# Segment sums of a chunked scan moved to TensorE with a constant triangle, and small work moved into the projections beside it

## Chip, cores and metric

The kernel runs on one core of a Trainium2 chip. The metric is device time in microseconds (us) for one launch; lower is better. The engines of the core that matter here are TensorE (PE), VectorE (DVE), ScalarE (ACT) and GpSimd (POOL). Each runs its own list of instructions in order, and they meet only at semaphores.

## What is computed

A float32 model of three residual layers over 512 tokens of width 1024: sparse attention with a gated MLP, a Mamba-2 scan mixer (SSD) with a gated MLP, and a short-convolution mixer with a gated MLP. The change lies in the scan mixer alone. Of the reference this is the part:

```python
def step(state, inp):                       # one chunk of 128 tokens; 4 chunks
    x_k, dt_k, b_k, c_k = inp               # 32 heads of 64, in 4 groups
    acs = jnp.cumsum(dt_k * a_g, axis=1)
    seg = acs[:, :, None] - acs[:, None, :]
    lmat = jnp.exp(jnp.where(causal, seg, -jnp.inf))
    cb = jnp.einsum("blgn,bsgn->blsg", c_k, b_k)
    w = cb[..., None] * lmat * dt_k[:, None]
    y = jnp.einsum("blsgh,bsghp->blghp", w, x_k)
    y = y + jnp.einsum("blgn,bghpn->blghp", c_k, state) * jnp.exp(acs)[..., None]
    decay = jnp.exp(acs[:, -1:] - acs) * dt_k
    state = (state * jnp.exp(acs[:, -1])[..., None, None]
             + jnp.einsum("bsgn,bsgh,bsghp->bghpn", b_k, decay, x_k))
    return state, y
```

Around it: `dt = softplus(dt_raw + dt_bias)`; `y` plus a skip term is multiplied by `silu(z)`, normalised over each of the 4 groups (512 channels, root of the mean square), scaled, and projected by `w_out`.

## The kernel before

Activations lie with channels on the 128 partitions and the 512 tokens in the free dimension. Each projection is a `gemm` over panels of weights. A weight panel is loaded by a DMA (`raw`), ACT copies it to the rounded type (`whi`, `weight_hi`), DVE takes the remainder (`wlo`, `weight_lo`), and PE multiplies in three products per block (L663 to L665). `SSD_IN` has 41 tiles; tile 24 (`DT_AT`) carries dt, whose softplus runs over the next tiles. Tiles 25 to 40 are the gate z. `SSD_OUT` takes 16 contraction blocks (its operand `yhi`, `ylo`), and its first two output tiles are multiplied block by block as those blocks become ready.

Between these two projections stands the scan. It has 16 steps G = 4c + g (chunk c, group g), each of 8 heads, handled as two halves U = 2G and 2G + 1 of 4 heads, 512 columns wide. The order on each engine is written out by hand. Per step:

- PE `spread(G)`: the product C·B of the group into bank 6 (L967), then for every head a matmul of dt·a, broadcast along the columns, with the triangle `usum` (L979), eight in all. It leaves in bank 0 or 1 the cumulative sum along the columns, the same in every row.
- DVE `segments(G)`: from each of these 128x128 blocks it subtracts the row's own cumulative sum and adds the mask `smask` (L1894, eight instructions).
- ACT: copies C·B to `cbuf` (L1363), takes the exponent of the spread sums for c > 0 (`xbuf`, L1370) and of the segments (`ebuf` or `sqr`, L1371).
- DVE `weights(G)`: multiplies the exponents by `cbuf` (L1906, two instructions).
- POOL: for c > 0 multiplies `xbuf` by C (L597, two instructions), and for c < 3 makes `xdec`, the decayed inputs (L606).
- PE `outputs(G)`: eight matmuls of `xdt` with the weights (L999), and for c > 0 eight of `state` with `xbuf` (L1002), two heads side by side in the array.
- PE `states(G)`, c < 3: one float32 matmul of 512 columns (L1013) into bank 7.
- DVE `gated(G)`: adds the skip term (L1917, four), multiplies by the gate (L1922), then waits for `states(G)` and updates `state` (L1929, or L1931 and L1934).
- ACT squares the result (L1355), PE sums the squares (`group_sums`, L1024).

Once per chunk PE turns x (`turn_x`, L949) into banks 0 to 3 and B (`turn_b`, L958) into bank 4, and DVE makes `xdt` (L1880). `turn_x(c + 1, ...)` thus shares banks with the spread sums and the outputs. The triangle and mask are made by POOL after `SSD_IN`. dt is turned (L925) and summed (L935, L936) on PE after the last tile of `SSD_IN`. After the last step all 16 group sums go through one mean, root and reciprocal (L1961, L1384, L1964), are spread over the partitions (L1060, 16 matmuls), and DVE and ACT make the operand blocks (L1974, L1387, L1968).

Of the kernel before, what the change touches and what calls it, by code (L numbers as in the profile page):

```python
# [213 lines left out]
def build(nc, w8, w22, xT, params, heads, w_cmp, w_ada, out):  # L214
    with ExitStack() as ctx:
# [89 lines left out]
        btok = sb("btok", [P, 4, P], F32, at(24))  # L305
        ebuf = sb("ebuf", [P, 2, S], F32, at(26))
        usum = sb("usum", [P, P], F32, at(30))
        smask = sb("smask", [P, P], F32, at(30.5))
# [102 lines left out]
        s_lb = sem("cumsums_spread")  # L411
        s_ein = sem("segments_made")
# [114 lines left out]
        def _(pool):  # L527
# [6 lines left out]
            chain(pool.memset(pcmp[:, :, :, :, :], 0.0))  # L534
            chain.wait()
            chain(pool.affine_select(out=ident[:, :], in_=ident[:, :], compare_op=ALU.not_equal, fill=1.0,
# [18 lines left out]
            def ada(half):  # L555

                for s in range(ADA_HALF * half, ADA_HALF * (half + 1)):
                    acc = ada_acc[:, s % 2, :]
                    for k in range(KD):
# [3 lines left out]
                        if k == 0:  # L563
                            if s >= 2:
# [14 lines left out]
            pool.wait_ge(s_pe, START["SSD_IN"] + 41)  # L579
            chain(pool.memset(usum[:, :], 1.0))  # L580
            chain(pool.memset(smask[:, :], 0.0))
            chain.wait()
            chain(pool.affine_select(out=usum[:, :], in_=usum[:, :], compare_op=ALU.is_ge, fill=0.0,
                                     base=0, pattern=[[1, P]], channel_multiplier=-1))
            chain(pool.affine_select(out=smask[:, :], in_=smask[:, :], compare_op=ALU.is_ge, fill=NEG,
                                     base=0, pattern=[[1, P]], channel_multiplier=-1))
            chain.wait()
            pool.memset(small[:, 31:32], 0.0).then_inc(s_const, 1)

            for c in range(NT):  # L590
                tok = slice(c * P, (c + 1) * P)
                for g in range(4):
                    for u in (2 * g, 2 * g + 1) if c else ():

                        pool.wait_ge(s_xe, 8 * (c - 1) + u + 1)
                        b = xbuf[:, u % 4, :].rearrange("p (a l) -> p a l", a=4)
                        pool.tensor_tensor(b, b, cv[:, 4 + g, tok].unsqueeze(1).to_broadcast([P, 4, P]),  # L597
                                           ALU.mult).then_inc(s_cx, 1)
                    if c < NT - 1:

                        pool.wait_ge(s_xd, 4 * c + g + 1)
                        pool.wait_ge(s_dec, 1)
                        if c > 0:
                            pool.wait_ge(s_st, 4 * (c - 1) + g + 1)
# [1560 lines left out]
```

## Time and profile before

| | us |
|---|---|
| median of 3 runs | 2294.11 (2292.66 to 2294.92) |
| the profiled execution | 2289.19 |
| its span, first to last instruction | 2287.5 |
| PE busy in the span | 2165.6 (95%) |
| DVE, ACT, POOL busy | 1309.2, 818.7, 293.2 |
| end of `SSD_IN` on PE to first block of `SSD_OUT` | 1019.8 to 1182.8 |

The profile has one execution. A busy PE is not a PE at its peak: the granted clock (PEclk, 1.00 is 2.4 GHz and 0.50 is 1.2 GHz) says how fast it was. A float32 matmul appears as two records, since it passes the array in two parts; "x16" records are thus eight matmuls. Matmuls overlap at their ends, so the distance from start to start tells what one costs. Idle time marked "issue" is a wait whose end the profile ties to no other engine.

### The profile page before, as it was taken

How to read it: one execution, taken by the hardware profiler on the slowest of the kernel's cores; microseconds unless marked ns; L12 is line 12 of the kernel's file. 1: busy time of each engine (PE TensorE's matmuls, PEld its weight loads, DVE VectorE, ACT ScalarE, POOL GpSimd, SP SyncE). 2: the span in 40 equal slices, each digit the busy share in tenths (PEclk: the TensorE clock that was granted, in tenths of full speed). 3: DMA queues.
4: the chain of work that ended last, by engine and by line, in shares of the span. 5: the costliest groups of instructions: out<-in, count | busy, mean ns of one | idle time of the engine just before them, and what ended most of it. 6: DMA issues, size and time to landing. Idle time of an engine off the chain costs nothing.

```text
span 2287.5 us, 27332 instructions
## 1 busy us (share of the span) xinstructions
PE 2165.6 (95%) x10704; PEld 1747.0 (76%) x10704; DVE 1309.2 (57%) x2222; ACT 818.7 (36%) x1324; POOL 293.2 (13%) x201
## 2 busy tenths in 40 slices
PE   7999988999999999997789999999989999999997
PEld 6866666888888778876678788888878877888885
DVE  4277754777754687638883587765455544333333
ACT  4156652544431354423242354442231223222221
POOL 0000000100049600002310200009800000000000
PEclk9999999999999999998899999999979988999998
DMA  8110002232245322220003122326512322222321
GB/s 272 50 47 20 20 10 65 84 101 92 93 150 200 116 96 102 92 93 1 1 1 111 65 102 93 100 86 212 192 47 92 101 65 73 93 92 94 94 92 53
DMA packets 59791, 203.58 MB, mean 89 GB/s; under 512 B 6800, under 2 KB 7312, under 8 KB 59408
## 3 DMA queue, kind: packets, MB, share of 16 engines
q1 hardware_dynamic: 55920, 191.36, 25.5%
q10 hardware_dynamic: 3744, 10.49, 1.4%
q8 instruction: 85, 1.39, 0.2%
q14 instruction: 42, 0.34, 0.0%
HBM read 197.63 MB, written 2.10 MB: 87 GB/s over the span
## 4 chain that ended last, share of the span: by engine, by line
PE 86%; DVE 6%; ACT 4%; issue 2%; POOL 1%; DMA 0%; DVEq 0%; SPq 0%; POOLq 0%; ACTq 0%
PE bank L663 25%; PE bank L664 25%; PE bank L665 25%; PE bank L618 2%; ACT pbuf L1244 2%; DVE pbuf L1681 1%; PE bank L766 1%; PE bank L861 1%; PE bank L815 1%; PE bank L838 1%; PE bank L645 1%; PE bank L979 1%; POOL h L553 1%; ACT pt L1261 1%; PE bank L1013 1%
## 5 line engine op out<-in xcount | busy, mean ns | idle before, releaser
L663 PE MATMUL bank<-xhi,whi 128*128 128x512 f32 x1712 | 685.6, 400 | 29.3 <-DVE xlo L1456 23.0
L664 PE MATMUL bank<-xlo,whi 128*128 128x512 f32 x1712 | 680.9, 398 | 0.0
L665 PE MATMUL bank<-xhi,wlo 128*128 128x512 f32 x1712 | 680.2, 397 | 0.0
L1444 DVE TENSOR_TENSOR wlo<-raw,whi 128x1024 fp32r<-128x1024 f32 (+1 forms) x322 | 412.6, 1283 | 367.8 <-ACT whi L1101 367.3
L1101 ACT ACTIVATE whi<-raw 128x1024 fp32r<-128x1024 f32 (+1 forms) x322 | 334.2, 1041 | 770.0 <-PE bank L665 709.5
L663 PEld LDWEIGHTS bank<-xhi,whi 128*128 128x128 f32 x1712 | 324.0, 189 | 110.7 <-issue 13.5
L665 PEld LDWEIGHTS bank<-xhi,wlo 128*128 128x128 f32 x1712 | 323.7, 189 | 79.8
L664 PEld LDWEIGHTS bank<-xlo,whi 128*128 128x128 f32 x1712 | 324.1, 189 | 77.0
L663 PE MATMUL bank<-hid_hi,whi 128*128 128x512 f32 x528 | 209.5, 397 | 0.0
L664 PE MATMUL bank<-hid_lo,whi 128*128 128x512 f32 x528 | 208.6, 395 | 0.0
L665 PE MATMUL bank<-hid_hi,wlo 128*128 128x512 f32 x528 | 208.5, 395 | 0.0
L665 PEld LDWEIGHTS bank<-hid_hi,wlo 128*128 128x128 f32 x528 | 99.0, 187 | 24.2
L663 PEld LDWEIGHTS bank<-hid_hi,whi 128*128 128x128 f32 x528 | 99.0, 188 | 23.9
L664 PEld LDWEIGHTS bank<-hid_lo,whi 128*128 128x128 f32 x528 | 99.0, 188 | 23.6
L571 POOL TENSOR_TENSOR ada_acc<-ada_acc,ada_w 128x768 f32<-128x768 f32 x56 | 115.8, 2069 | 4.7
L1560 DVE TENSOR_TENSOR upad<-bank,rstd_b 128x512 f32<-128x512 f32 x88 | 60.6, 691 | 78.3 <-PE bank L665 71.2
L553 POOL TENSOR_TENSOR h<-tmp,h 128x512 f32<-128x512 f32 x24 | 38.0, 1619 | 493.2 <-DVE tmp L1487 493.2
L1159 ACT ACTIVATE tmp<-upad,par 128x512 f32<-128x512 f32 x88 | 70.5, 803 | 27.0 <-DVE upad L1560 26.9
L1244 ACT ACTIVATE pbuf<-pbuf,stat 128x512 f32<-128x512 f32 (+3 forms) x128 | 70.2, 551 | 24.7 <-DVE stat L1684 24.7
L566 POOL TENSOR_SCALAR ada_acc<-ada_w,csil 128x768 f32<-128x768 f32 x8 | 12.2, 1527 | 510.3 <-DMA ada_w<-w_ada 510.3
L568 POOL TENSOR_SCALAR ada_w<-ada_w,csil 128x768 f32<-128x768 f32 x56 | 75.0, 1340 | 0.8 <-DMA ada_w<-w_ada 0.8
L1572 DVE SCALAR_TENSOR_TENSOR tmp<-upad,par,tmp 128x512 f32<-128x512 f32 x88 | 66.2, 752 | 3.1
(269 smaller groups left out, 2558.8 us busy)
## 6 DMA issues: line engine op xcount, KB each, us to landing
raw<-w SPq DMA_DIRECT2D x298, 512.0 KB, 3.6
ada_w<-w_ada SPq DMA_DIRECT2D x64, 384.0 KB, 3.1
raw<-w SPq DMA_DIRECT2D x24, 384.0 KB, 3.4
h<-xT ACTq DMA_DIRECT2D x8, 256.0 KB, 9.7
w_k<-w_cmp ACTq DMA_DIRECT2D x1, 2048.0 KB, 9.6
w_v<-w_cmp ACTq DMA_DIRECT2D x1, 2048.0 KB, 8.2
out_t<-h ACTq DMA_DIRECT2D x8, 256.0 KB, 2.0
dk<-stg ACTq DMA_DIRECT2D x2, 256.0 KB, 6.9
```

Of the source, the lines that this page charges most:

```text
L553: pool.tensor_tensor(h[:, j, :], tmp[:, j % 2, :], h[:, j, :], ALU.add).then_inc(s_h, 1)
L568: chain(pool.tensor_scalar(w, w, csil[:, k:k + 1], 1.0, ALU.mult, ALU.mult))
L571: pool.tensor_tensor(acc, acc, w, ALU.add).then_inc(s_ada_k, 1)
L663: pe.matmul(bk, whi[w][:, cols], hi[:, k, :], start=k == 0, stop=False)
L664: pe.matmul(bk, whi[w][:, cols], lo[:, k, :], start=False, stop=False)
L665: return pe.matmul(bk, wlo[w][:, cols], hi[:, k, :], start=False, stop=last)
L1101: act.activation(whi[g % SLOTS][:, 0:n], raw[g % RAWS][:, 0:n], ACT.Copy).then_inc(s_hi, 1)
L1159: act.activation(tmp[:, c % 2, :], upad[:, c % 2, 2:2 + S], ACT.Identity, scale=col("ffn_w", 3 * k + 2), bias=col("ffn_b", k)).then_inc(s_ ...
L1244: act.activation(pbuf[:, s % 3, g, 0:n], pbuf[:, s % 3, g, 0:n], ACT.Exp, scale=QSCALE, bias=stat[:, b, 4 + g:5 + g], accum_out=stat[:, b, ...
L1444: dve.tensor_tensor(wlo[g % SLOTS][:, 0:n], raw[g % RAWS][:, 0:n], whi[g % SLOTS][:, 0:n].bitcast(F32), ALU.subtract).then_inc(s_lo, 1)
L1560: dve.tensor_tensor(upad[:, c % 2, 2:2 + S], in_bank(c)[:, :], rstd_b[:, :], ALU.mult)\
L1572: ins = dve.scalar_tensor_tensor(out=tmp[:, v, :], in0=upad[:, v, 0:S], scalar=col("ffn_w", 3 * k), in1=tmp[:, v, :], op0=ALU.mult, op1=AL ...
```

## The change

- Segments on PE. ACT now writes the terms (`terms`): for each head the constant triangle `usum` times that head's dt·a, a copy with a per-partition scale, eight 128x128 instructions per step into four buffers `vbuf`. One matmul with the constant strictly lower triangle `after` turns the terms of four heads, 512 columns, into finished segments (`segments`, L985 in the new file). For c > 0 a second matmul of the same terms with `ones` gives the spread cumulative sums (`spread_cumsums`, L991).
- DVE loses the eight segment instructions; masking moves into C·B, which DVE multiplies by `usum` while copying it to `cbuf` (`causal_cb`, one 128x128 instruction). ACT loses that copy.
- x is turned step by step, two steps ahead, into bank 4 alone, and B into the same bank; B has two buffers. `keep_state` is a step of its own after `x_dt(G + 2)`. `gated(G)` comes in step G instead of a step later, and writes over `cv` rather than `tmp`.
- dt: `turn_dt` stands before tile 32 of `SSD_IN`, `cumulate` before tile 35, and DVE's copies of them between its tiles. The constants are made by POOL at the start of the kernel.
- Group norm: groups 0 to 2 are finished first; the sum of the last step, and the spread of group 3, are put before contraction blocks 4 and 8 of `SSD_OUT`.
- POOL's work per step is the same, with `xdec` ahead of the products with C.

PE, the last step of chunk 0 and what leads to chunk 1. `ident,cv` are the turns of x and B, `xdec,btok` the state products. Before:

```order
L999 MATMUL bank<-ebuf,xdt 64x128 x8
L1013 MATMUL bank<-xdec,btok 128x512
L1024 MATMUL bank<-ones,tmp 128x1 x4
L949 MATMUL bank<-ident,cv 128x128 x8
L999 MATMUL bank<-sqr,xdt 64x128 x8
L967 MATMUL bank<-cv 128x128
L979 MATMUL bank<-usum,dtk 128x128 x8
L1013 MATMUL bank<-xdec,btok 128x512
L949 MATMUL bank<-ident,cv 128x128 x8
L958 MATMUL bank<-ident,cv 128x128 x4
```

And now, one step:

```order
L985 MATMUL bank<-vbuf_122,after 128x512
L985 MATMUL bank<-vbuf_123,after 128x512
L1030 MATMUL bank<-ones,tmp 128x1 x4
L1008 MATMUL bank<-sqr,xdt 64x128 x8
L991 MATMUL bank<-vbuf_122,ones 128x512
L991 MATMUL bank<-vbuf_123,ones 128x512
L964 MATMUL bank<-ident,cv 128x128 x4
L974 MATMUL bank<-cv 128x128
L1021 MATMUL bank<-xdec,btok_117 128x512
```

Eight narrow matmuls became two of 512 columns, two more of 512 columns came in, and the turns are spread one group a step, behind the outputs.

DVE, two steps of chunk 1. `ebuf`/`sqr` times `cbuf` are the weights. Before:

```order
L1894 SCALAR_TENSOR_TENSOR ebuf<-bank,acs,smask 128x128 x8
L1917 SCALAR_TENSOR_TENSOR tmp<-cv,par,bank 128x128 x4
L1922 TENSOR_TENSOR zb<-zb,tmp 128x4x128
L1931 TENSOR_TENSOR state<-state,acs 128x512
L1934 TENSOR_TENSOR state<-state,bank 128x512
L1906 TENSOR_TENSOR ebuf<-ebuf,cbuf 128x512 x2
L1894 SCALAR_TENSOR_TENSOR sqr<-bank,acs,smask 128x128 x8
```

And now, one step:

```order
L1954 TENSOR_TENSOR ebuf<-ebuf,cbuf 128x512 x2
L1964 SCALAR_TENSOR_TENSOR cv<-cv,par,bank 128x128 x4
L1968 TENSOR_TENSOR zb<-zb,cv 128x4x128
L1938 TENSOR_TENSOR xdt<-bank,dtk 128x512
L1945 TENSOR_TENSOR cbuf<-bank,usum 128x128
```

The eight segment instructions are gone; one narrow one and one turn's `xdt` came in, and the weights stand ahead of the gate instead of behind the state.

The diff, cut to its core (removed functions are printed above):

```diff
--- before.py
+++ after.py
...
+        after = sb("after", [P, P], F32, at(130))
+        vbuf = [sb("vbuf0", [P, S], F32, where["ssum"]), sb("vbuf1", [P, S], F32, at(127.5)),
+                sb("vbuf2", [P, S], F32, at(124.25)), sb("vbuf3", [P, S], F32, at(120))]
...
-            gemm("SSD_IN", xhi, xlo, s_ev, EV["SSD_IN"], Q_SSD_PRE, freed=out_ring_left("DOWN1"))
...
+            gemm("SSD_IN", xhi, xlo, s_ev, EV["SSD_IN"], Q_SSD_PRE, freed=out_ring_left("DOWN1"),
+                 between=[((DT_AT + 8, 0), turn_dt), ((DT_AT + 11, 0), cumulate)])
...
+                if g == 0 and c < NT - 1:
+                    pe.wait_ge(s_bt, c + 1)
+                elif G:
+                    pe.wait_ge(s_xd, G)
...
-                for v in range(2):
...
-                    for k in range(4):
-                        hd = 8 * g + 4 * v + k
-                        mm = pe.matmul(bank[v][:, k * P:(k + 1) * P],
-                                       dtk[:, c, 1, hd:hd + 1].to_broadcast([P, P]), usum[:, :],
-                                       start=True, stop=True)
-                    mm.then_inc(s_lb, 1)
+            def segments(G):
+                for U in (2 * G, 2 * G + 1):
+                    pe.wait_ge(s_vm, U + 1)
+                    if U >= 10:
+                        pe.wait_ge(s_xe, U - 2 - 8 + 1)
+                    elif U >= 2:
+                        pe.wait_ge(s_ee, U - 1)
+                    pe.matmul(bank[U % 2][:, :], after[:, :], vbuf[U % 4][:, :], start=True, stop=True).then_inc(s_lb, 1)
+            def spread_cumsums(G):
+                for U in (2 * G, 2 * G + 1):
+                    pe.wait_ge(s_ee, U + 1)
+                    pe.matmul(bank[U % 2][:, :], ones[:, :], vbuf[U % 4][:, :], start=True, stop=True).then_inc(s_lx, 1)
...
+            for G in range(4 * NT):
+                c, g = G // 4, G % 4
+                if G + 1 < 4 * NT:
+                    segments(G + 1)
+                if G >= 2:
+                    if G == 2:
+                        pe.wait_ge(s_acv, 1)
+                    group_sums(G - 2)
+                outputs(G)
+                if G + 1 < 4 * NT and G + 1 >= 4:
+                    spread_cumsums(G + 1)
+                if G + 2 < 4 * NT:
+                    if g == 2 and c + 1 < NT - 1:
+                        turn_b(c + 1)
+                    turn_x(G + 2)
+                    products_cb(G + 2)
+                if c < NT - 1:
+                    states(G)
+            group_sums(4 * NT - 2)
+            pe.wait_ge(s_gn, 2)
+            pe.wait_ge(s_xe, 8 * (NT - 1))
+            pe.wait_ge(s_ee, 8 * NT)
+            pe.wait_ge(s_xd, 4 * NT)
+            for g in range(3):
+                spread_group(g)
+            pe.wait_ge(s_yk, 4 * NT)
...
+            def last_sums():
+                group_sums(4 * NT - 1)
+            def last_spread():
+                pe.wait_ge(s_gn, 4)
+                spread_group(3)
+            gemm("SSD_OUT", yhi, ylo, s_m, MV["SSD_OUT"], post=Q_SSD_POST, freed=[[]] * 4,
+                 between=[((None, 4), last_sums), ((None, 8), last_spread)])
...
+            def terms(G):
+                c, g = G // 4, G % 4
+                for v in range(2):
+                    U = 2 * G + v
+                    if U >= 12:
+                        act.wait_ge(s_lx, U - 4 - 8 + 1)
+                    elif U >= 4:
+                        act.wait_ge(s_lb, U - 4 + 1)
+                    for k in range(4):
+                        hd = 8 * g + 4 * v + k
+                        ins = act.activation(vbuf[U % 4][:, k * P:(k + 1) * P], usum[:, :], ACT.Copy,
+                                             scale=dtk[:, c, 1, hd:hd + 1])
+                    ins.then_inc(s_vm, 1)
...
+            def segment_exps(G):
+                for U in (2 * G, 2 * G + 1):
+                    act.wait_ge(s_lb, U + 1)
+                    if U >= 4:
+                        act.wait_ge(s_y, U - 3)
+                    act.activation(segs(U), bank[U % 2][:, :], ACT.Exp).then_inc(s_ee, 1)
...
+            terms(0)
+            keep_b(0)
+            segment_exps(0)
+            terms(1)
...
+                if G + 1 < 4 * NT:
+                    segment_exps(G + 1)
+                if G + 2 < 4 * NT:
+                    terms(G + 2)
+                if G + 1 < 4 * NT and G + 1 >= 4:
+                    cumsum_exps(G + 1)
+                if g == 2 and c + 1 < NT - 1:
+                    keep_b(c + 1)
+                if G >= 1:
+                    group_square(G - 1)
+            act.activation(small[:, 13:14], small[:, 12:13], ACT.Sqrt)
...
+            act.activation(gst[:, 1, 0:12], gst[:, 0, 0:12], ACT.Sqrt).then_inc(s_gr, 1)
             for j in range(NZ):
+                if j == 6:
+                    act.wait_ge(s_gn, 3)
+                    act.activation(gst[:, 1, 12:16], gst[:, 0, 12:16], ACT.Sqrt).then_inc(s_gr, 1)
...
+                if c == DT_AT + 9:
+                    dve.wait_ge(s_dtp, 1)
...
+                if c == DT_AT + 12:
+                    dve.wait_ge(s_ac, 1)
...
-            def segments(G):
...
-                    for k in range(4):
-                        hd = 8 * g + 4 * v + k
-                        ins = dve.scalar_tensor_tensor(
-                            out=segs(U)[:, k * P:(k + 1) * P], in0=bank[v][:, k * P:(k + 1) * P],
-                            scalar=acs[:, 0, c, hd:hd + 1], in1=smask[:, :], op0=ALU.subtract, op1=ALU.add)
-                    ins.then_inc(s_ein, 1)
+            def causal_cb(G):
+                dve.wait_ge(s_cb, G + 1)
+                dve.tensor_tensor(cbuf[:, G % 2, :], bank[6][:, 0:P], usum[:, :], ALU.mult).then_inc(s_cbk, 1)
...
+            dve.wait_ge(s_dtk, 1)
+            x_dt(0)
+            causal_cb(0)
+            causal_cb(1)
             weights(0)
+            x_dt(1)
+            dve.wait_ge(s_cv, 40)
             dve.wait_ge(s_dec, 1)
             for G in range(4 * NT):
...
+                if G + 1 < 4 * NT:
                     weights(G + 1)
-                    continue
-                gated(G - 1)
+                gated(G)
+                if G + 2 < 4 * NT:
+                    x_dt(G + 2)
+                    causal_cb(G + 2)
                 if c < NT - 1:
-                    x_dt(c + 1, 0)
...
+                    keep_state(G)
...
+            mean_squares(slice(0, 12), 4 * NT - 1)
+            inverse_roots(slice(0, 12), 1)
             for j in range(NZ):
                 g = j // 4
+                if j == 5:
+                    mean_squares(slice(12, 16), 4 * NT)
+                if j == 8:
+                    inverse_roots(slice(12, 16), 2)
```

## Rows read from the trace of the kernel before

**Rows 1.** Windows of the scan: us, busy us per engine, PEclk, DMA share, GB/s
```profile
1021.00:1030.00 9.00, 7.20 (x39) 7.23 (x40) 5.10 (x9) 2.29 (x4) 3.07 (x4) 0.67 0.17 61
1030.00:1060.00 30.00, 24.11 (x195) 20.42 (x193) 25.06 (x70) 7.96 (x16) 1.07 (x2) 0.93 0.00 1
1060.00:1097.00 37.00, 27.17 (x224) 23.19 (x224) 30.31 (x62) 12.02 (x24) 16.73 (x12) 0.82 0.00 1
1097.00:1138.00 41.00, 30.11 (x233) 25.34 (x232) 33.93 (x71) 12.30 (x25) 16.72 (x12) 0.82 0.00 1
1138.00:1175.00 37.00, 29.34 (x291) 26.49 (x291) 30.21 (x70) 12.98 (x27) 10.89 (x8) 0.92 0.00 1
```

**Rows 2.** Timeline in chunk 1: start, duration, instruction, [idle before and releaser]
```profile
1076.41 0.69 DVE L1934 TENSOR_TENSOR state<-state,bank 128x512 f32<-128x512 f32 x1
...
1077.20 2.05 PE L1013 MATMUL bank<-xdec,btok 128*128 128x512 f32 x2 [5.79 <-issue]
```

**Rows 3.** Waits between 1021 and 1183: waiting <- releaser: us, times, longest
```profile
PE bank L1013 <- issue: 25.1, 6, 5.8
```

**Rows 4.** Timeline of PE where it ran at the full clock without waiting
```profile
1097.05 0.49 PE L967 MATMUL bank<-cv 128*128 128x128 f32 x2
...
1097.37 1.95 PE L979 MATMUL bank<-usum,dtk 128*128 128x128 f32 x16
...
1099.16 1.02 PE L1013 MATMUL bank<-xdec,btok 128*128 128x512 f32 x2
...
1100.02 1.04 PE L949 MATMUL bank<-ident,cv 128*128 128x128 f32 x8
...
1101.33 0.95 PE L1024 MATMUL bank<-ones,tmp 128*128 128x1 f32 x8
...
1162.16 0.45 PE L999 MATMUL bank<-ebuf,xdt 128*64 128x128 f32 x4 [1.31 <-DVE zb L1922]
...
1164.09 1.05 PE L1024 MATMUL bank<-ones,tmp 128*128 128x1 f32 x8
```

**Rows 5.** Timeline from the end of SSD_IN to the first outputs
```profile
1019.51 0.40 PE L665 MATMUL bank<-xhi,wlo 128*128 128x512 f32 x1
...
1021.60 1.28 ACT L1347 ACT_TABLE_LOAD   x1
...
1022.80 0.38 PE L935 MATMUL bank<-dtk,usum 128*128 128x32 f32 x2 [2.28 <-DVE dtk L1860]
...
1034.71 1.09 PE L999 MATMUL bank<-ebuf,xdt 128*64 128x128 f32 x16
```

**Rows 6.** ACT: two scaled copies in a row (timeline), and a narrow plain one (groups)
```profile
8.68 0.71 ACT L1192 ACTIVATE xhi<-h,par 128x512 fp32r<-128x512 f32 x1
9.29 1.04 ACT L1101 ACTIVATE whi<-raw 128x1024 fp32r<-128x1024 f32 x1
...
L1363 ACT ACTIVATE cbuf<-bank 128x128 f32<-128x128 f32 x16 | 4.4, 272 | 16.4 <-PE bank L967 16.4
```

**Rows 7.** DVE in the scan by tile: count, ns minimum/median/maximum, first and last start
```profile
L1894 DVE SCALAR_TENSOR_TENSOR sqr<-bank,acs,smask x64: 335/340/351, 1034.9 to 1164.3; 128x128 f32<-128x128 f32 x64
L1880 DVE TENSOR_TENSOR xdt<-bank,dtk x16: 677/682/692, 1026.3 to 1150.6; 128x512 f32<-128x512 f32 x16
L1906 DVE TENSOR_TENSOR sqr<-sqr,cbuf x16: 677/686/1755, 1036.9 to 1167.9; 128x512 f32<-128x512 f32 x16
L1922 DVE TENSOR_TENSOR zb<-zb,tmp x16: 691/692/1659, 1041.6 to 1172.6; 128x512 f32<-128x512 f32 x16
L1931 DVE TENSOR_TENSOR state<-state,acs x8: 684/1109/1526, 1074.8 to 1144.1; 128x512 f32<-128x512 f32 x8
```

**Rows 8.** The end of the scan: timeline, then two groups by tile
```profile
1171.33 1.05 PE L1024 MATMUL bank<-ones,tmp 128*128 128x1 f32 x8
...
L663 PE MATMUL bank<-yhi,whi x128: 393/396/477, 1182.8 to 1272.7; 128*128 128x512 f32 x128
...
L1974 DVE SCALAR_TENSOR_TENSOR zb<-zb,par,bank x16: 740/744/751, 1179.8 to 1198.2; 128x512 f32<-128x512 f32 x16
```

More of the change, by code:

```diff
@@ L534, in _ @@
             chain(pool.memset(pcmp[:, :, :, :, :], 0.0))
+            chain(pool.memset(usum[:, :], 1.0))
+            chain(pool.memset(after[:, :], 1.0))
             chain.wait()
+            chain(pool.affine_select(out=usum[:, :], in_=usum[:, :], compare_op=ALU.is_ge, fill=0.0,
+                                     base=0, pattern=[[1, P]], channel_multiplier=-1))
+            chain(pool.affine_select(out=after[:, :], in_=after[:, :], compare_op=ALU.is_ge, fill=0.0,
+                                     base=-1, pattern=[[-1, P]], channel_multiplier=1))
             chain(pool.affine_select(out=ident[:, :], in_=ident[:, :], compare_op=ALU.not_equal, fill=1.0,
@@ L578, in _ @@
             add_update(KD)
[L579 to L596, printed above, removed]
+            for n in range(-1, 4 * NT):
+                c, g = (n + 1) // 4, (n + 1) % 4
+                if c >= NT:
+                    continue
+                if c < NT - 1:
+                    pool.wait_ge(s_xd, n + 2)
+                    pool.wait_ge(s_dec, 1)
+                    if c:
+                        pool.wait_ge(s_st, n - 2)
+                    hs = slice(8 * g, 8 * g + 8)
+                    pool.tensor_tensor(xdec[:, hs, :], xdt[:, hs, :],
+                                       acs[:, 1, c, hs].unsqueeze(2).to_broadcast([P, 8, HD]),
+                                       ALU.mult).then_inc(s_xdec, 1)
+                if c:
+                    tok = slice(c * P, (c + 1) * P)
+                    for U in (2 * n + 2, 2 * n + 3):
+                        pool.wait_ge(s_xe, U - 8 + 1)
+                        b = xbuf[:, U % 4, :].rearrange("p (a l) -> p a l", a=4)
@@ L688, in gemm @@
                             continue
+                        for (t, at_block), extra in between:
+                            if t is None and at_block == off + kb:
+                                extra()
                         pe.wait_ge(s_xt, XT[name] + off + kb + 1)
@@ L700, in gemm @@
                 for t in range(lead, n):
+                    for (tile, _), extra in between:
+                        if tile == t:
+                            extra()
                     bank_free(t)
@@ new lines, in cumulate @@
+            def cumulate():
+                pe.wait_ge(s_dtk, 1)
+                for c in range(NT):
+                    dta = dtk[:, c, 1, :]
+                    pe.matmul(bank[5][:, c * SH:(c + 1) * SH], usum[:, :], dta, start=True, stop=True)
+                    mm = pe.matmul(bank[5][:, (NT + c) * SH:(NT + c + 1) * SH], ones[:, :], dta, start=True, stop=True)
+                mm.then_inc(s_ac, 1)
+            gemm("SSD_IN", xhi, xlo, s_ev, EV["SSD_IN"], Q_SSD_PRE, freed=out_ring_left("DOWN1"),
+                 between=[((DT_AT + 8, 0), turn_dt), ((DT_AT + 11, 0), cumulate)])
```

249 lines of the change are left out of this document (82 added, 167 removed).

## Prediction

> **What bounds the kernel now.** I read the time by stage first, then the waits inside the stage that changes, then single instructions. Outside the scan PE is busy at the full clock and nothing of the change lies there but small pieces. From the end of `SSD_IN` (1019.8) to the first block of `SSD_OUT` (1182.8) the kernel spends 163.0 us. There PE is busy 24.1 of 30, 27.2 of 37, 30.1 of 41 and 29.3 of 37 us, at a granted clock of 0.93, 0.82, 0.82 and 0.92, while DVE is busy 25 to 34 us of each [rows 1]. So DVE's chain sets the pace and PE pays twice: it waits, and behind a wait it runs at half rate. In [rows 2] the reader sees one such place. PE idled 5.79 us ahead of the state product L1013, whose turn came when DVE had finished the state of the group before (1076.41 + 0.69 = 1077.10), and the product then took 2.05 us at the 1.2 GHz level, where the same pair takes 1.02 at 2.4 [rows 4]. These waits are 25.1 us in all, six of them [rows 3]; the clock behind them costs more. First outputs begin at 1034.7 [rows 5], the last end at 1171.3 [rows 8]: 136.6 us for 16 steps, 8.5 us a step.
>
> **What DVE loses.** Per step 8 segment instructions of 0.34 (start to start 0.27), 2.2 us, go [rows 7]. One narrow product with the triangle comes in, 0.29 as I estimate from the 0.34 row. Left are two weights 2 x 0.68, gate about 1.1 + 0.69, `xdt` 0.68, `causal_cb` 0.29, state 0.68 in chunk 0 or 0.69 + 0.69 later [rows 7]: 4.8 us in chunk 0 and 5.5 in chunks 1 and 2.
>
> **What ACT gains.** Eight 128x128 copies with a scale per partition. The narrow plain copy lasts 0.272. The scaled one of 512 columns lasts 0.71 and lets the next start after 0.61 [rows 6]. So each costs between 0.17 (0.27 less the 0.10 of overlap) and 0.37 (0.27 plus 0.10 for the scale, no overlap); I take 0.27, nearest to the narrow row: 2.2 us a step, bounds 1.4 and 3.0. With two exponents (0.6 each, four in c > 0) and the square, ACT works 4.1 us a step in chunk 0 and 5.3 later, 6.1 at the upper bound.
>
> **What PE does now.** Start-to-start costs at full clock [rows 4]: C·B 0.32; old spread sums 1.79; state product 0.86 (0.9 with the gap behind it); four turns 0.87 to 0.95; square sums 0.95; outputs 1.93 in c > 0, and 1.09 in chunk 0 [rows 5]. A float32 matmul of 512 columns is the same form as L1013, so the two segment matmuls are 1.8, as dear as the eight they replace. The two with `ones` in c > 0 are new: 1.8 x 12 steps = 21.6 us more PE work. Summed by the new order, from the start of the first outputs:
> steps 0 to 3: 3.3 (its segments are before it), 5.1, 7.0 (with one turn of B), 7.8 (spread sums of step 4 begin);
> steps 4 to 11: 1.8 + 0.95 + 1.95 + 1.8 + 0.95 + 0.32 + 0.9 = 8.67 each, with one more turn of B 70.3;
> steps 12, 13: 7.77 each; step 14: 6.5; step 15: 2.9.
> Together 118.4 us. Known waits on top: two turns that wait for ACT to copy B (0.8 each), and the last outputs, which follow their own spread sums by only 0.95 us while ACT and POOL still have to work on them, 1.0. That is 121.0.
>
> **Does anything else stop PE?** Through one step of 8.67: segments end at 1.8; ACT's exponents at 2.5, its terms for the next step at 4.7 (5.5), which PE wants at 8.67; outputs end at 4.7; spread sums at 6.5, exponents at 7.1, wanted free at 8.67; POOL's products with C end near 9.2, wanted at 11.4. DVE: weights by 3.3, gate 4.8 to 6.6, `xdt` behind the turn (7.5) to 8.2, state behind its product (8.7) to 10.2, next weights wanted much later. All other engines have one to three us in hand. So PE is the bound and has no gap of over about 1 us. Its clock then is 1.00; I take that because the windows without such gaps have it.
>
> **The start.** The last `SSD_IN` matmul moves back by the two pieces put between tiles, 2.3 us (today 1022.80 to 1025.1 for the sums [rows 5], part of it at half rate). In exchange the wait of 2.28 on DVE is gone. But ACT's last gate tile, its table load of 1.28 [rows 5] and the exponent of the sums now stand ahead of `terms(0)`: 1025.6, first terms 1026.8, second 1027.9. PE has idled about 4 us and gets half rate, as it did after 1022 (0.67 in [rows 1]): segments 1026.9 to 1030.4, turn to 1032.2, `xdt`, `causal_cb`, second C·B, weights, and the next segments, first outputs at 1036.5. That is 1.8 us later than now. Were the clock full, it would be 1034 to 1035.
>
> **The end.** Last outputs at 1036.5 + 121.0 = 1157.5, against 1171.3. Today 11.5 us follow until `SSD_OUT` begins. Two rounds of square and sum (the sum is 1.05 [rows 8]) and one of four spreads go from ahead of it, near 4 us earlier. It is given back: at block 4 PE sums the last step's squares (0.95), DVE stands waiting for that sum before block 5 and only then makes the remainder of block 4, so PE stalls about 1.7; the last spread costs 0.9. DVE makes a block in (1198.2 - 1179.8)/15 = 1.23 and PE takes 1.41 for one (two output tiles, from 128 triples in 89.9 us) [rows 8], so DVE does not catch the stall up, and PE does not stall again. 4 - 3.5 is 0 to 1; I put 0. POOL's constants at the kernel's start are hidden by the first weight load.
>
> **Sum.** 2289.19 - 13.8 = 2275.4 us for an execution like the profiled one. The median shown is 4.9 above it, 0.2%; so 2294.1 - 13.8 = 2280.3.
> The terms' bounds: start -1.8 to +1; gaps between PE's groups 0 instead of 3.7; waits 0 to 5; end -2 to +2. That is a gain of 8 to 21.
>
> **Rivals.**
> A: POOL takes DVE's time. Two-input operations from SBUF stretch when POOL works: the weights to 1.76, gate product to 1.66, state to 1.53, while the segments, which read PSUM, never passed 0.351 [rows 7]. The change removes just those that do not stretch. Fully stretched a step of chunks 1 and 2 is 2 x 1.76 + 1.1 + 1.66 + 0.68 + 0.29 + 1.53 + 0.69 = 9.5, with two handovers 9.8, 1.1 over PE's 8.67: 8 x 1.1 = 9, a gain of only 5, 2289. Against it: POOL is busy 4.2 of 8.67 us. The Trainium skill, GPSIMD Engine Reference, section Specifications, says that GpSimd's SBUF interfaces are shared with VectorE and contended by instructions with two SBUF inputs; the trace agrees.
> B, the other side: PE gets its added 21.6 us of work but not the clock. If the grant stays at the 0.87 that the four windows average today, 118.4/0.87 + 2.6 = 138.7 from 1036.5, so 1175.2, 4 us later than now: 2298. It decides at 0.90. For it: today the scan never held 1.00 over a whole window. Against it: the low stretches stand behind waits of 3 to 6 us, and the new order has none after the start. The Trainium skill, TensorE: Matmul & The Clock Gate, section HAM oscillation, has it that idle gaps throttle the array; by that rule the time is my 2280, and the trace agrees in [rows 2].
> C: more than forecast, PE's groups closer and the start at full clock: 2273 and below.
>
> **Chances.** Forecast (2272 to 2286) 0.66; A (2286 to 2293) 0.17; B (above 2293) 0.09; C 0.08. A difference of 0.2%, 4.6 us, is about what a measurement of this kernel can tell. Faster than 2289.5 are the forecast, C and half of A: 0.82; same 0.10; slower 0.08. Range 2271 to 2291, which leaves out B and most of C.
>
> **What would show it.** Right: windows of chunks 1 to 3 with PE busy over 95% at a clock of 1.00; 8.7 us from one state product to the next; the wait ahead of the state product gone; DVE waiting for PE's outputs and states; scaled copies near 0.27 apart; one stall of about 1.7 us before block 5 of `SSD_OUT`. Wrong: PE waiting for weights (A), windows under 0.9 (B), ACT's terms ending after PE asked for them, or a first output later than 1038.

## The result

The changed kernel takes 2269.35 us in the median of 4 runs (2265.03 to 2270.14), beside 2293.7 for the kernel before on the same chip: a ratio of 0.989, 95% interval 0.9876 to 0.9904. That is 24.4 us less, where 13.8 were forecast, and 1.7 below the low end of the range. The profiled execution took 2270.14 us with a span of 2268.4, against 2289.19 and 2287.5 before.

**Which difference of the two traces to trust.** The spans differ by only 19.1. In the trace of after the first product of `NSA_OUT` begins at 342.9, before at 337.2, and of the change only POOL's constants lie ahead of it. In the 14 traces of this study that start lies between 336.9 and 343.3, and variants of the changed kernel stand at both ends, so 6 us of scatter arise ahead of it and sit in every span. I therefore read a distance that leaves it out, from the first product of a `DOWN` stage to the last. The rows give the minimum, median and maximum ns and the first and last start. After:

```profile
L664 PE MATMUL bank<-hid_hi,whi x528: 393/396/479, 652.7 to 2250.2; 128*128 128x512 f32 x176
```

and the same tile in the kernel before:

```profile
L663 PE MATMUL bank<-hid_hi,whi x528: 393/396/479, 648.3 to 2269.1; 128*128 128x512 f32 x176
```

1620.8 us before and 1597.5 after: 23.3 less, close to the 24.4 of the medians. Below, "distance" is this number. It has a scatter of its own: the stretch from the last `SSD_OUT` product to the last `DOWN` product, in which no kernel here differs, takes 995.4 to 998.0 in the 14 traces, and there is one trace of each kernel. What is worth 1 or 2 us I read from the stages below, and not from the distance alone.

**By stage**, from the same landmarks in both traces (before by [rows 5, 8]):

| stretch | before | on record | after |
|---|---|---|---|
| first `DOWN` product to last `SSD_IN` product | 371.2 | 373.5 | 373.8 |
| to the first outputs | 15.2 | 14.7 | 13.3 |
| first outputs to the end of the last outputs | 136.6 | 121.0 | 110.1 |
| to the first `SSD_OUT` product | 11.5 | 7.5 | 7.4 |
| first to last `SSD_OUT` product | 89.9 | 93.4 | 94.9 |
| to the last `DOWN` product, nothing changed | 996.4 | | 998.0 |

The large miss is in one row, the scan: 26.5 us less instead of 15.6. The changed stages together are 24.9 less; the last row gives 1.6 of it back by scatter.

**What bounds it after.** The windows answer to [rows 1]: us, busy us per engine, PEclk, DMA share, GB/s.

```profile
1020.00:1040.00 20.00, 15.10 (x58) 9.76 (x58) 6.96 (x11) 11.88 (x27) 1.11 (x2) 0.83 0.22 72
1040.00:1060.00 20.00, 18.90 (x131) 12.35 (x129) 17.65 (x38) 16.05 (x45) 5.26 (x5) 1.00 0.00 1
1060.00:1130.00 70.00, 69.26 (x500) 46.39 (x499) 51.08 (x94) 46.39 (x117) 31.00 (x25) 1.00 0.00 1
1130.00:1150.00 20.00, 18.80 (x153) 13.01 (x152) 9.86 (x23) 11.75 (x24) 7.47 (x6) 1.00 0.00 1
```

From 1060 to 1130, chunks 1 and 2 and the start of chunk 3, PE is busy 69.3 of 70 us at a granted clock of 1.00, DVE 51.1, ACT 46.4. The wait ahead of the state product, 25.1 us in [rows 3], is gone; the waits now run the other way (waiting <- releaser: us, times, longest):

```profile
DVE cv L1964 <- PE bank L1011: 17.4, 12, 4.3
...
ACT xbuf L1402 <- PE bank L991: 14.9, 23, 3.2
DVE xdt L1938 <- PE bank L964: 13.9, 12, 7.0
...
PE bank L985 <- ACT vbuf L1384: 4.3, 1, 4.3
```

One step of chunk 1, PE's timeline, which answers to [rows 4]:

```profile
1060.74 1.88 PE L985 MATMUL bank<-vbuf,after 128*128 128x512 f32 x4
1062.46 0.95 PE L1030 MATMUL bank<-ones,tmp 128*128 128x1 f32 x8
1063.34 0.45 PE L1008 MATMUL bank<-ebuf,xdt 128*64 128x128 f32 x4
...
1065.29 1.98 PE L991 MATMUL bank<-vbuf,ones 128*128 128x512 f32 x4
1067.11 0.60 PE L964 MATMUL bank<-ident,cv 128*128 128x128 f32 x4
1067.55 0.39 PE L974 MATMUL bank<-cv 128*128 128x128 f32 x2
1067.77 1.02 PE L1021 MATMUL bank<-xdec,btok 128*128 128x512 f32 x2
```

State products stand 7.88 apart (the next is at 1075.65), not 8.67. Read start to start: segments 1.72, sums 0.88, outputs 1.95, spreads with `ones` 1.82, turn **0.44**, C·B 0.22, state product 0.86. The turn is the only term that is off by more than 0.1. Its row ends in x4, four records for four tiles. The sums' row ends in x8 for four products, C·B's in x2 for one. A float32 product leaves two records, a transposing one leaves one.

### The profile page after: what moved, and what is told of

It is laid out like the page before. It is cut to its first block, busy times and chain, and to the rows that moved or that the text cites. A ratio compares the mean times of both kernels' runs of the same rounds, so it can differ in the third digit from the quotient of the medians.

```text
span 2268.4 us, 27014 instructions
## 1 busy us (share of the span) xinstructions
PE 2174.0 (96%) x10560; PEld 1728.7 (76%) x10560; DVE 1269.9 (56%) x2112; ACT 854.4 (38%) x1438; POOL 289.4 (13%) x200
## 4 chain that ended last, share of the span: by engine, by line
PE 90%; DVE 5%; ACT 4%; issue 1%; POOL 1%; DMA 0%; SPq 0%; DVEq 0%; ACTq 0%; POOLq 0%
PE bank L664 25%; PE bank L665 25%; PE bank L666 25%; PE bank L619 2%; ACT pbuf L1268 1%; PE bank L985 1%; PE bank L774 1%; PE bank L869 1%; DVE pbuf L1740 1%; PE bank L991 1%; PE bank L823 1%; PE bank L846 1%; PE bank L646 1%; PE bank L1008 1%; ACT pt L1285 1%
## 5 line engine op out<-in xcount | busy, mean ns | idle before, releaser
L1125 ACT ACTIVATE whi<-raw 128x1024 fp32r<-128x1024 f32 (+1 forms) x322 | 334.2, 1040 | 773.3 <-PE bank L666 706.1
L575 POOL TENSOR_SCALAR ada_acc<-ada_w,csil 128x768 f32<-128x768 f32 x8 | 12.2, 1524 | 509.4 <-DMA ada_w<-w_ada 509.4
```

What stands on the lines that cost most here:

```text
L1125: act.activation(whi[g % SLOTS][:, 0:n], raw[g % RAWS][:, 0:n], ACT.Copy).then_inc(s_hi, 1)
```

## The experiments

Medians of 4 runs (5 in one case) stand beside the kernel before on the same chip; `after` has no run of its own there, so I put it at 2269.4. The kernel before stood at 2293.6 to 2295.4 beside these runs and at 2293.7 beside `after`, so up to 1.7 us of a difference to 2269.4 can be the chip's.

### Is the turn the mis-sized term?

Every turn issued twice (the edit for x; B's is alike):

```diff
-                for k in range(4):
+                for k in (0, 1, 2, 3, 0, 1, 2, 3):
                     mm = pe.transpose(bank[4][:, k * P:(k + 1) * P],
...
```

> Every turn of four tiles in the scan is issued twice, 16 turns of x and 3 of B; the rest is the changed kernel (2269.4 us). My theory now: PE bounds the scan and a turn costs 0.44 us on it (1067.11 to 1067.55 in the trace of after), so 19 x 0.44 = 8.4 us more, 2277.8, and the state products stand 8.3 us apart instead of 7.88. The term on record, 0.95 for a turn, gives 18 us more, 2287. Rival: not PE but a ring of waits over ACT and DVE sets the step of 7.88; then the turns fall into slack, 0 to 2 us more.

Measured: 2274.9 us (ratio 0.9906, 0.9891 to 0.9921), 5.5 more; distance 1604.5, 7.0 more. PE in chunk 1:

```profile
1066.22 1.98 PE L991 MATMUL bank<-vbuf,ones 128*128 128x512 f32 x4
1068.04 1.04 PE L964 MATMUL bank<-ident,cv 128*128 128x128 f32 x8
1068.92 0.39 PE L974 MATMUL bank<-cv 128*128 128x128 f32 x2
1069.14 1.02 PE L1021 MATMUL bank<-xdec,btok 128*128 128x512 f32 x2
...
1077.46 1.02 PE L1021 MATMUL bank<-xdec,btok 128*128 128x512 f32 x2
```

Eight turns take 1068.92 - 1068.04 = 0.88, and the state products stand 8.32 apart: 0.44 more, as expected. From `SSD_IN` to the end of the last outputs it is 8.4 us more, the 8.4 expected; `SSD_OUT` was 1.6 shorter (93.3), so the sum shows less. PE pays for what it is given, and a turn is worth 0.44. The row has the x8 and the 1.04 of L949 in [rows 4]; that was two turns, and I had priced it as one.

The same turns as plain products with the identity (again x's edit, B's is alike):

```diff
-                    mm = pe.transpose(bank[4][:, k * P:(k + 1) * P],
-                                      cv[:, 8 + 4 * g + k, c * P:(c + 1) * P], ident[:, :])
+                    mm = pe.matmul(bank[4][:, k * P:(k + 1) * P],
+                                   cv[:, 8 + 4 * g + k, c * P:(c + 1) * P], ident[:, :],
+                                   start=True, stop=True)
```

> The changed kernel with every turn of x and B in the scan made as a plain product with the identity instead of a transposing one: the same 76 instructions of 128 columns. Theory: the term on record, 0.87 to 0.95 for four, is the price of four plain products (4 x 0.22 = 0.88 by the old spread sums), and a transposing one costs half. So 19 x (0.88 - 0.44) = 8.4 us more, 8.3 us from one state product to the next, and 2277.8: most of the way to the 2280.3 on record. Rival: the forms cost the same and the 0.44 is a matter of what stands around them; then 2269.

Measured: 2278.0 us (0.9926, 0.9907 to 0.9945); distance 1606.0, 8.5 more. PE:

```profile
1067.63 1.98 PE L993 MATMUL bank<-vbuf,ones 128*128 128x512 f32 x4
1069.45 1.05 PE L965 MATMUL bank<-ident,cv 128*128 128x128 f32 x8
1070.34 0.39 PE L976 MATMUL bank<-cv 128*128 128x128 f32 x2
```

Four plain products take 0.89 where four transposing ones take 0.44. A kernel with turns at the price I recorded takes 2278, inside the recorded range and 2.3 us from the recorded time. The Trainium skill bears on this in "TensorE: Matmul & The Clock Gate", section Terms: trn2's transpose mode is said to be four times as fast for FP32. I did not weigh that sentence of the skill, which spoke for a cheaper turn. Here the factor is 2, 0.89 to 0.44, and the measurement decides.

### Is PE the bound, and how far is the next engine?

Spreads with `ones` over a quarter of the columns:

```diff
-                    pe.matmul(bank[U % 2][:, :], ones[:, :], vbuf[U % 4][:, :], start=True, stop=True).then_inc(s_lx, 1)
+                    pe.matmul(bank[U % 2][:, 0:P], ones[:, :], vbuf[U % 4][:, 0:P], start=True, stop=True).then_inc(s_lx, 1)
```

> The 24 products with ones that spread the cumulated sums stream 128 instead of 512 columns; three quarters of what is exponentiated behind them is then stale, a part of the computation left out. PE has 24 x 0.65 = 15.5 us less to do. PE is the bound: the step of 7.88 falls by 1.3 to 6.6 in chunks 1 to 3, still over DVE's 5.8 and ACT's 5.3 of busy time a step, and the time is 2254. Rival: the step is set by the ring segments - exponents - weights - outputs, or DVE with its handovers is close behind (over 7.2 a step): a gain of under 8 us, 2262 or more.

Measured: 2252.8 us (0.9813, 0.9796 to 0.9829), 16.6 less; distance 1581.2, 16.3 less. Of that the scan gave 14.2, for the 15.5 us of work taken away; the step is 6.61, and DVE was busy 61.1 of 65 us from 1060 to 1125. So PE bounds the changed kernel, and with 1.3 us less a step DVE is close behind.

Twice the scaled copies on ACT, every second one into a spare tile:

```diff
...
+                        act.activation(spare[:, k % 2, :], usum[:, :], ACT.Copy,
+                                       scale=dtk[:, c, 1, hd:hd + 1]).then_inc(s_sp, 1)
```

> Each scaled copy on ACT is followed by one more into a spare tile, 8 x 0.29 = 2.3 us more work a step, all else as in the changed kernel (2269.4). Theory: ACT is busy 5.2 of 7.9 us a step, so 7.6 still fit; only the exponents behind the terms come later, 0 to 5 us in all, up to 2274. Rival: ACT stands right behind PE in the ring, and the copies come through one for one: 16 x 2.3 less the slack of 0.3, 2290 and more.

Measured: 2281.0 us (0.9944, 0.9929 to 0.9959); distance 1611.1, 13.6 more: neither. The windows:

```profile
1028.00:1062.00 34.00, 21.20 (x111) 11.34 (x112) 16.35 (x35) 31.53 (x95) 4.17 (x4) 0.92 0.05 16
1062.00:1140.00 78.00, 75.60 (x499) 48.15 (x499) 61.09 (x100) 67.11 (x191) 35.20 (x26) 0.97 0.00 1
```

In chunks 1 to 3 the copies did fit, but for 3.6 us (PE busy 75.6 of 78). In chunk 0 a PE step is only 4.4 us and ACT works 31.5 of 34: state products stand 6.2 apart there, and PE waits 3.4 once for ACT's copy of B. I had averaged ACT's slack over stages with different limits. In the changed kernel itself DVE is the second engine of chunks 0 to 2, and ACT that of chunk 3 (11.8 us to DVE's 9.9, 1130 to 1150). DVE is nearest to being the bound in chunk 0, where the windows from 1040 to 1052 have it busy 11.9 of 12 us, ACT 10.7 and PE 11.1. The middle one is:

```profile
1044.00:1048.00 4.00, 4.00 (x28) 2.52 (x28) 3.97 (x10) 3.63 (x12) 1.04 (x1) 1.00 0.00 0
```

### What did the move between the engines bring, and what the order?

The changed order with the segments on DVE again, no terms, no `ones`:

```diff
-                    act.activation(segs(U), bank[U % 2][:, :], ACT.Exp).then_inc(s_ee, 1)
+                    act.activation(segs(U), segs(U), ACT.Exp).then_inc(s_ee, 1)
...
+                        ins = dve.scalar_tensor_tensor(
+                            out=segs(U)[:, k * P:(k + 1) * P], in0=bank[U % 2][:, k * P:(k + 1) * P],
+                            scalar=acs[:, 0, c, hd:hd + 1], in1=after[:, :], op0=ALU.subtract, op1=ALU.add)
```

> The changed kernel in all but the move of the segments: the same order of the groups, the same places of dt, norm, turns and state, but DVE makes the segments from the spread sums again (8 x 0.27 = 2.2 us a step), ACT copies no terms, PE has one set of spreads and no products with ones. Theory: DVE's work is the bound and the engine move is the gain; 4 steps of 7.1, 8 of 8.4 and 4 of 6.5 make 121.6 us in place of 110.1, so 2281, with PE waiting for weights. Rival: the new order and the smaller banks of waits made the gain, since PE has 1.8 us less to do here: 2265 to 2272.

Measured: 2285.7 us (0.9966, 0.9953 to 0.9979); distance 1615.9, only 4.9 less than before, 18.4 more than the changed kernel. By the distance the order, with the two smaller moves, brings a fifth of the gain and the move of the segments the rest; by the medians (8.9 us less than the kernel before beside it, of 24.4) it is over a third. The traced run was the slowest of the five, which makes the distance the lower of the two. In the scan alone, 133.7 us stand between 136.6 before and 110.1 after. The window of chunk 1:

```profile
1060.00:1090.00 30.00, 19.76 (x192) 16.48 (x192) 29.83 (x58) 8.98 (x17) 13.61 (x10) 0.95 0.01 1
```

and DVE's timeline in it:

```profile
1068.55 3.43 DVE L1942 TENSOR_TENSOR sqr<-sqr,cbuf 128x512 f32<-128x512 f32 x2
...
1072.70 1.55 DVE L1968 TENSOR_TENSOR state<-state,acs 128x512 f32<-128x512 f32 x1
```

DVE is busy 29.8 of 30 us. The time is 4.7 above what I expected, and the scan 12 above (133.7 for 121.6); a start 3 us shorter than in the changed kernel hides part of that. I had taken the weights at 2 x 0.68 and a step at 8.4. Here a pair took 3.43 and the state product 1.55, and DVE's steps are 10.2 apart. These are the instructions that rival A said would stretch, [rows 7]; that POOL's work is what stretches them is likely from the trace, but no run took POOL's work away.

The kernel before with idle products in PE's six long waits:

```diff
+                for _ in range({1: 12, 2: 11, 5: 23, 6: 14, 9: 23, 10: 14}.get(G, 0)):
+                    pe.matmul(bank[5][:, 3 * P:4 * P], usum[:, :], ident[:, :], start=True, stop=True)
                 pe.wait_ge(s_xdec, G + 1)
```

> The kernel before, with idle products of 0.22 us each (a triangle with the identity, into an unused quarter of the statistics' bank) put on PE ahead of the six state products that waited 2.7 to 5.8 us: 12, 11, 23, 14, 23 and 14 of them. They fill the waits and change nothing that is computed. Theory: PE ran at half rate behind its waits, and that lay on the path; by the windows some 10 to 14 us of the 136.6 are the clock. Then the windows of the scan show a clock of 1.00 and the kernel before gets 6 to 14 us faster, 2280 to 2288 against 2294. Rival: DVE's chain sets the end whatever the clock, and faster products only wait longer: within 2 us of 2294.

Measured: 2279.1 us (0.9941, 0.9924 to 0.9957), 15.5 less than the kernel before beside it (13.5 by the ratio); distance 1609.4, 11.4 less. It computes the same and has 97 products more. Where [rows 2] had a wait of 5.79 and a state product of 2.05:

```profile
1071.88 5.40 PE L1010 MATMUL bank<-ident,usum 128*128 128x128 f32 x46
1077.74 1.10 PE L1015 MATMUL bank<-xdec,btok 128*128 128x512 f32 x2 [0.46 <-issue]
```

and the windows, to be read beside the 0.82 of [rows 1]:

```profile
1060.00:1090.00 30.00, 28.13 (x266) 25.03 (x265) 27.60 (x59) 11.25 (x23) 16.70 (x12) 1.00 0.00 1
1090.00:1120.00 30.00, 28.44 (x274) 25.28 (x274) 26.81 (x58) 10.22 (x22) 12.76 (x9) 1.00 0.00 1
```

So PE's half rate behind its waits cost the kernel before some 11 to 15 us, about half of what the change brought. Not all of it is gone: from 1130 to 1160 the clock is still 0.90. DVE's chain sets the end, but it passes through PE's products, and these were slow just when DVE needed them.

### The two smaller moves

The turning and cumulating of dt behind `SSD_IN` again:

```diff
...
-                 between=[((DT_AT + 8, 0), turn_dt), ((DT_AT + 11, 0), cumulate)])
...
+            turn_dt()
+            cumulate()
...
```

> The turning and cumulating of dt stand behind SSD_IN again, the rest is the changed kernel. The step on record: the two pieces cost SSD_IN 2.3 us and save the 2.3 us wait on DVE, a plain exchange, so the time stays within 1.5 us of 2269.4. Rival: they also take the whole chain turn, copy, sums, two copies, difference, exponent off the path to the first terms: without them the first outputs begin 3 to 5 us later against a shorter SSD_IN, 2271 to 2273.

Measured: 2268.5 us (0.9884, 0.9869 to 0.9899); distance 1597.9, 0.4 more. No difference that can be told: `SSD_IN` ends earlier, and the first outputs come 17.2 us behind it instead of 13.3. PE then waited 2.2 for `dtk` and 1.7 for the first terms. The move is the exchange on record.

The group norm in one piece again:

```diff
...
-                 between=[((None, 4), last_sums), ((None, 8), last_spread)])
+            gemm("SSD_OUT", yhi, ylo, s_m, MV["SSD_OUT"], post=Q_SSD_POST, freed=[[]] * 4)
...
```

> The group norm is in one piece ahead of SSD_OUT again, the rest is the changed kernel. The step on record: the split is an exchange, near 4 us before SSD_OUT against 1.7 + 0.95 + 0.9 in it, so 2269.4 within 1.5 us. Rival: the stall at block 4 with the half clock behind it (0.77 to 0.81 from 1164 to 1172 in the trace of after) makes the split a loss: this kernel is 1 to 2 us faster, and the 89.9 us of SSD_OUT before are back in place of 94.9.

Measured: 2266.6 us (0.9876, 0.9861 to 0.989); distance 1595.9, 1.6 less. `SSD_OUT` is back at 89.9 us and starts 3.5 us later behind the last outputs. So the split costs 5.0 - 3.5 = 1.5 us by the stages. The distance agrees; the medians, 2.8 apart, allow it. In the changed kernel (PE's timeline at block 4):

```profile
1162.98 0.95 PE L1030 MATMUL bank<-ones,tmp 128*128 128x1 f32 x8
1165.44 0.50 PE L664 MATMUL bank<-yhi,whi 128*128 128x512 f32 x1 [1.51 <-DVE ylo L2006]
...
1168.19 0.63 PE L666 MATMUL bank<-yhi,wlo 128*128 128x512 f32 x1
```

The stall was forecast at 1.7 and is 1.51. Behind it eight products stand 0.43 apart instead of 0.23; that is the missing 1.5.

### From the readings to a better version

The spreads with `ones` as turns of a broadcast column:

```diff
-                    pe.matmul(bank[U % 2][:, :], ones[:, :], vbuf[U % 4][:, :], start=True, stop=True).then_inc(s_lx, 1)
+                    for k in range(4):
+                        hd = 4 * (U % 8) + k
+                        mm = pe.transpose(bank[U % 2][:, k * P:(k + 1) * P],
+                                          acs[:, 0, U // 8, hd:hd + 1].to_broadcast([P, P]), ident[:, :])
+                    mm.then_inc(s_lx, 1)
```

> The 24 products with ones (0.86 us each) are replaced by 96 turns of one broadcast column of the cumulated sums, the same numbers. If a turn of 128 columns costs 0.11 us with a broadcast operand too, PE has 12 x (1.79 - 0.44 x 2) = 10.9 us less to do; PE being the bound the time is 2258.5, with 7.0 us between state products. Rival: the broadcast operand makes a turn as dear as the old spread matmul, 0.22 each: no change, 2269.

Measured: 2257.5 us (0.9843, 0.9829 to 0.9858), 11.9 less; distance 1587.0, 10.5 less. The eight turns:

```profile
1071.57 1.09 PE L993 MATMUL bank<-ident,acs 128*128 128x128 f32 x8
1072.49 0.60 PE L964 MATMUL bank<-ident,cv 128*128 128x128 f32 x4
1072.93 0.39 PE L974 MATMUL bank<-cv 128*128 128x128 f32 x2
```

0.92 for eight in place of 1.82, and 6.99 from state product to state product. PE held a clock of 1.00 from 1060 to 1130 with 12 turns a step, some 1.4 of 7 us. The Trainium skill, "TensorE: Matmul & The Clock Gate", Part 4: PE-mode transpose, says that the full clock does not engage for transpose mode. At this share of turns the trace does not show that, and no run here has a stretch of turns alone.

All small terms together (cut to its kinds of edits):

```diff
+                if c == 40:
+                    act.wait_ge(s_dtk, 1)
+                    terms(0)
+                    terms(1, 0, 1)
...
-            group_square(4 * NT - 1)
             act.wait_ge(s_gn, 1)
             act.activation(gst[:, 1, 0:12], gst[:, 0, 0:12], ACT.Sqrt).then_inc(s_gr, 1)
+            group_square(4 * NT - 1)
...
-                 between=[((None, 4), last_sums), ((None, 8), last_spread)])
+                 between=[((None, 4), last_sums), ((None, 9), last_spread)])
```

> The version the readings point to. From the changed kernel: cumulated sums and group roots are spread by turns (spread_turned: 12 us), ACT makes the first three halves of the terms in its 4 us wait ahead of the last SSD_IN tile instead of behind it, its square stands ahead of the last exponents, the state product stands between the turn of B and that of x, and the remainder of the group norm has its sums, root, inverse and spread one to two blocks later in SSD_OUT. Theory, PE the bound with no wait left in it: start 4 to 6 us earlier, waits on btok (1.8) and on the square (1.2) gone, 3 us from the group spreads, stall at block 4 with its half clock (1.5 + 1.5) gone: 2257.5 - 12 = 2245. Rival: the first outputs hang on ACT's exponents behind its table load, and the norm's chain over DVE, ACT and DVE ahead of SSD_OUT is as long as before: 2251 to 2254.

Measured: 2246.1 us (0.9796, 0.978 to 0.9812); distance 1576.6, 20.9 less than the changed kernel. It is faster than the changed kernel and than `spread_turned`. The first outputs stand 8.2 us behind `SSD_IN`, since the first terms are made in a wait of ACT's; the stall at block 4 is gone. One new loss shows at the end, where PE waits for POOL and then runs at half rate (its timeline, then the window):

```profile
1125.74 0.45 PE L1012 MATMUL bank<-sqr,xdt 128*64 128x128 f32 x4 [1.46 <-POOL xbuf L608]
...
1131.39 2.82 PE L1041 MATMUL bank<-ident,gst 128*128 128x128 f32 x12 [0.77 <-DVE gst L2031]
```

```profile
1126.00:1140.00 14.00, 12.66 (x64) 10.70 (x61) 9.58 (x19) 5.05 (x10) 0.71 (x1) 0.52 0.00 1
```

Idle products in the waits of the changed kernel, and in those three:

```diff
             pe.wait_ge(s_ev, EV["UP2"])
+            idle(18)
             segments(0)
...
```

> The changed kernel with idle products (0.22 us each) on PE in two waits: 18 in the 4.3 us ahead of the first segments, 10 in the 2 us ahead of the group spreads. Theory, the clock behind a wait lies on the path here too: segments at 1.88 in place of 3.75 and what follows them at the start near 2.5 us, the group spreads 4.47 to 2.9, together 3 to 4 us, 2266. Rival: at the start ACT's table load, exponents and terms bring the first outputs at 1039.9 whatever PE's clock, and only the 1.5 us at the end remain: 2268.

> next_version (2246.1) with idle products in the three waits at its end: 7 ahead of the last outputs (wait of 1.46), 9 ahead of the group spreads, 8 ahead of SSD_OUT. There PE ran from 1126.2 to 1140 at a granted clock of 0.52. Theory: the clock stays at 1.00; the last outputs, the last sums, the spreads and the first block of SSD_OUT then take 5 to 7 us less, 2240. Rival: DVE and ACT pace this stretch (gate, root, inverse, two blocks), PE only gets longer waits: 1 us, 2245.

Measured: `after_filled` 2265.3 us (0.9879, 0.9862 to 0.9895), distance 1592.3, 5.2 less; segments at the start took 2.01, not 3.75, and the first outputs stand 11.4 us behind `SSD_IN`. `next_filled` 2246.3 us (0.9793, 0.9779 to 0.9808), the same time as without; its distance is 1573.9, 2.7 less, at a clock of 1.00 from 1128 to 1142. That gain is below what the medians can tell; I had expected 5 to 7. Where DVE and ACT hand one small result to the other, as at this end, a full clock on PE brought only part of what PE's own times promised.

## Why the prediction was wrong, and what of it was right

**What bounded the kernel before: right, and stronger than I put it.** "PE pays twice" was the right reading: filling the waits with idle work alone brought 11 to 15 us. I gave the clock no price of its own in the text.

**What PE does now: this step failed.** "Four turns 0.87 to 0.95" is wrong; they take 0.44. I read x8 in L949's row [rows 4] as four tiles of two records each, which is how the float32 products beside it count. My sentence that a float32 matmul appears as two records holds for plain products, not for transposing ones. PE's timeline of the kernel before had the row that tells, the four tiles of B:

```profile
1059.04 0.60 PE L958 MATMUL bank<-ident,cv 128*128 128x128 f32 x4
```

Four tiles, four records, and the next row begins 0.43 behind it, at 1059.47. Sixteen turns lie in the sum of 118.4, so 16 x 0.51 = 8.2 of the 10.9 us. The rest are terms a little too high: C·B 0.32 for 0.22 (14 x 0.1 = 1.4), sums 0.95 for 0.88 (14 x 0.07 = 1.0; 0.95 is the row's duration, not the distance from start to start), segments 1.8 for 1.72 (14 x 0.08 = 1.1), state product 0.9 for 0.86 (12 x 0.04 = 0.5). Together 12.2, less 0.4 by which the waits were longer, so 11.8 for the 10.9 measured; about 1 stays unexplained. The experiments show the turn's part; the small ones are only read from the rows, and why C·B and the segments cost less behind a full PE is open.

**Waits in the scan: right in size, one by another cause.** Two for the copies of B, 1.10 and 0.74 (forecast 0.8 each). The last outputs came 1.20 late, but because PE stood at the sums of step 13 until ACT's square, which ACT had queued behind the last exponents (1147.00, idle 1.20 before it). POOL's products, which I named, ended at 1148.13, just ahead of PE's first product with them at 1148.25; that the size came out near 1.0 is luck. With the square moved, in `next_version`, POOL is what PE waits for.

**Does anything else stop PE: right for chunks 1 to 3.** DVE and ACT had 2 us a step. In chunk 0 I never set DVE's 4.8 and ACT's 4.1 beside a PE step of that chunk. That came to 4.41 without square sums, and DVE took 4.63 for its own, so DVE was falling behind until the sums (0.88) joined PE's steps. The scaled copies start 0.29 apart, forecast 0.27.

**The start: 1.4 us too late.** First outputs 13.3 behind `SSD_IN` for the 14.7 forecast. Each stage was as told (the wait of 4.28, segments at half rate 3.75), but what lies between these and the first outputs, two turns and two C·B among it, took 4.7 for the 6.1 forecast. The sign "a first output later than 1038" did come in this trace (1039.8), but 4.4 us of that stand ahead of the first `DOWN` product (652.7 for 648.3).

**The end: 1.5 us too good.** The 4 us ahead of `SSD_OUT` and the stall of 1.51 are as written. What was missing is the half rate behind the stall, the very effect that I named for the scan. The two errors, start and end, cancel in the sum.

**Rivals.** A: the stretching is there (the state product with the decay has a median of 1.34, in [rows 7] 1.11), but DVE has the room in chunks 1 to 3; it became the bound there only in `segments_on_dve`. B is refuted: the clock is 1.00 over 110 us. C, "PE's groups closer and the start at full clock", named the side on which the time fell but not the cause: the start was at half rate, and the groups were closer by less than the turn.

**The range** had gaps "0 instead of 3.7" as its only term below the sum of PE's work. It had no bound for a price itself being wrong by half, and that was the case. Nor do its own terms give "8 to 21": at their favourable ends they add 2.8 + 3.7 + 2.6 + 2 = 11.1 to the 13.8, so 24.9, and at the other ends they take 2.4 + 2 off, so 9.4. The 3.7 stands in no row. That 24.9 is near the 24.4 measured says nothing, since no term in it is the one that failed.

## What to carry over

Where PE is to become the bound, the forecast is a plain sum of its instructions, so settle each price with two rows of different counts, and ask how many records one instruction leaves; a transposing product costs half of a plain float32 one here and can also replace a product with `ones` or a broadcast column. A long wait of PE cost its length and the half rate behind it here, also when another engine set the pace: price both, or try idle products in the wait, which is a one-line experiment. When spans scatter by several us, measure from one landmark behind the scatter to another, and measure a stretch that nothing changes as well: it tells how small a difference you may believe.

## What the runs showed of the hardware

- A float32 turn of 128 columns: 0.11 start to start, one record; a plain float32 product of the same shape 0.22, two records. A broadcast column as the turned operand costs no more (0.92 for eight).
- In `before_filled` idle products of 128 columns held the granted clock at 1.00 from 1060 to 1120, where waits of up to 5.8 us had stood, and the kernel with 97 of them more was 11 to 15 us faster.
- Half rate followed a single wait of 1.46 us in `next_version` and one of 1.51 in the changed kernel, but not the waits of 0.75 and 0.83 at the start of `next_version`, nor one of 1.71 in `terms_twice` (1.00 from 1098 to 1106). The length of the wait alone did not decide it.
- Eight scaled copies of 128 columns on ACT take 2.43 us, 0.29 each from start to start and 0.39 from start to end; the narrow plain copy took 0.27 from start to end [rows 6].
